# Attention on one core: scores of two tiles in one batch, and the shares divided by their sums in rows on GpSimd

## What is computed

```python
for window, dilation in DILATED_PATTERNS:      # (128, 1), (512, 4), (2048, 16)
    o_i, lse_i = dilated_window_attn(q, k, v, window, dilation)
    ...
mix_w = jax.nn.softmax(jnp.stack(lses, axis=0), axis=0)
o = jnp.sum(mix_w[..., None] * jnp.stack(outs, axis=0).astype(jnp.float32), axis=0)
attn_out = o.astype(x.dtype).reshape(B, S, ATTN_WIDTH) * jax.nn.silu(g_attn)
```

## Time and profile before

| | |
|---|---|
| median of 3 runs | 2517.62 us (2516.89 to 2519.19) |
| the profiled execution's own time | 2515.38 us |
| its span, first to last instruction | 2513.4 us |
| busy in the span: PE, DVE, ACT, POOL | 97%, 51%, 44%, 25% |
| attention, first score product to last gate | from 479.66 us, last gate starts at 609.45 us and takes 0.69 us |
| busy from 480 to 600 us: PE, DVE, ACT, POOL | 118.85, 72.48, 79.35, 42.16 us of 120 |

### The profile page before, as it was taken

One profiled execution on the slowest core, in us unless ns is written; L12 is line 12 of the kernel. 1 busy time (PEld: TensorE's weight loads), 2 busy tenths in 40 slices (PEclk: granted clock), 3 DMA queues, 4 the chain that ended last, 5 costly groups with the idle time before them and its releaser, 6 DMA issues. The chain is left out here.

```text
span 2513.4 us, 31851 instructions
## 1 busy us (share of the span) xinstructions
PE 2439.6 (97%) x12866; PEld 2019.2 (80%) x12866; DVE 1285.0 (51%) x1582; ACT 1097.3 (44%) x1569; POOL 616.2 (25%) x497
## 2 busy tenths in 40 slices
PE   8899999999999999999999998999999999999997
PEld 7788888766878788888888777877888888888885
DVE  5654102254521312213554286335269998888985
ACT  5510221365333121121422265233237877877783
POOL 0121232142412122133231056314111114312100
PEclk9999999999999999999999999999999999999999
DMA  7732321242232113113242374222548999999996
GB/s 287 271 107 84 107 75 54 89 129 83 92 101 67 34 34 134 51 59 127 68 134 59 126 276 175 102 70 67 182 186 365 386 377 396 393 384 376 379 376 242
DMA packets 138299, 446.47 MB, mean 178 GB/s; under 512 B 20952, under 2 KB 63640, under 8 KB 121512
## 3 DMA queue, kind: packets, MB, share of 16 engines
q1 hardware_dynamic: 96304, 380.23, 40.5%
q0 software_dynamic: 15632, 36.29, 3.9%
q10 hardware_dynamic: 26216, 27.89, 3.4%
HBM read 385.06 MB, written 77.14 MB: 184 GB/s over the span
## 5 line engine op out<-in xcount | busy, mean ns | idle before, releaser
L3220 DVE TENSOR_TENSOR ex_w_lo<-ex_w,ex_w_hi 128x2048 fp32r<-128x2048 f32 x198 | 447.4, 2289 | 55.0 <-ACT ex_w_hi L3156 53.7
L3156 ACT ACTIVATE ex_w_hi<-ex_w 128x2048 fp32r<-128x2048 f32 x198 | 376.9, 1916 | 34.6 <-DMA ex_w<-w 19.8
L249 POOL TENSOR_TENSOR p_w_lo<-w_raw,p_w_hi 128x512 fp32r<-128x512 f32 (+1 forms) x138 | 181.7, 1348 | 593.2 <-ACT p_w_hi L275 592.4
L316 PE MATMUL p_ps<-hT_hi,p_w_hi 128*128 128x512 f32 (+1 forms) x608 | 218.7, 360 | 3.5 <-DVE p_w_lo L249 3.3
L317 PE MATMUL p_ps<-hT_lo,p_w_hi 128*128 128x512 f32 (+1 forms) x608 | 217.3, 357 | 0.0
L318 PE MATMUL p_ps<-hT_hi,p_w_lo 128*128 128x512 f32 (+1 forms) x608 | 217.2, 357 | 0.0
L275 ACT ACTIVATE p_w_hi<-w_raw 128x512 fp32r<-128x512 f32 (+1 forms) x200 | 112.4, 607 | 218.3 <-PE p_ps L318 88.2
L249 POOL TENSOR_TENSOR p_w_lo_rest<-w_raw,p_w_hi_rest 128x512 fp32r<-128x512 f32 x64 | 86.8, 1391 | 207.1 <-ACT p_w_hi_rest L275 207.1
L316 PEld LDWEIGHTS p_ps<-hT_hi,p_w_hi 128*128 128x128 f32 x608 | 116.1, 191 | 21.4 <-DVE hT_lo L715 3.4
L318 PEld LDWEIGHTS p_ps<-hT_hi,p_w_lo 128*128 128x128 f32 x608 | 116.0, 191 | 16.3
L317 PEld LDWEIGHTS p_ps<-hT_lo,p_w_hi 128*128 128x128 f32 x608 | 116.0, 191 | 16.2
(11 more groups left out here) (525 smaller groups left out, 6005.2 us busy)
## 6 DMA issues: line engine op xcount, KB each, us to landing
ex_w<-w SPq DMA_DIRECT2D x99, 2048.0 KB, 14.5
w_raw<-w_in SPq DMA_DIRECT2D x36, 1024.0 KB, 5.2
w_raw<-w_xkv_panels SPq DMA_DIRECT2D x8, 1024.0 KB, 7.0
w_raw<-w_out SPq DMA_DIRECT2D x8, 1024.0 KB, 8.6
x_rows<-o_x SPq DMA_DIRECT2D x16, 512.0 KB, 2.6
qk_columns<-ml_qk_first ACTq DMA_DIRECT2D x16, 512.0 KB, 3.2
w_raw<-w_qk_panels SPq DMA_DIRECT2D x6, 1024.0 KB, 7.7
plain_cols<-x SPq DMA_DIRECT2D x8, 512.0 KB, 7.3
```

Source lines behind the costliest of these rows:

```text
L249: emit(self.lo(n)[:, 0:w], self.half(n // (KC // 2), w)[:, n % (KC // 2), :], self.hi(n)[:, 0:w].bitcast(F32), ALU.subtract).then_inc(self ...
L316: pe.matmul(out, a, x, start=start, stop=False)
L3156: nc.scalar.activation(w_hi[:, n % RING, :], raw_half(n), ACT.Copy).then_inc(hi_done, 1)
L3220: nc.vector.tensor_tensor(w_lo[:, n % RING, :], raw_half(n), w_hi[:, n % RING, :].bitcast(F32), ALU.subtract).then_inc(down_lo if m == "w2 ...
```

## The change

Two things are changed in attention.

First, steps of kind "rows" now cover two tiles (n and n + 1). TensorE makes the near products of both tiles and then the far products of both. The steps stand at other places: ahead of units 0 and 1 for tiles 4-5 and 6-7, ahead of units 3 and 4 for tiles 0-1 and 2-3 of the next pair.

Second, the kind "sums" is gone, with spread_sums, keep_scales, scale, and the buffer att_scales (its place in memory stays taken, so nothing else moves). Each tile's shares are instead divided in rows: invert takes the reciprocals of two tiles, 4 columns at a time, and a new function normalize on GpSimd multiplies each row of att_sc by its reciprocal, in place, four instructions for two tiles. turn waits for them (normed) instead of for the exponentials (expd).

```diff
+    NORMED_BEHIND = {1: HALF, 2: HALF + 2, 4: NT, 6: NT + 2}
...
-        for a in range(HALF):
+        for a in range(0, HALF, 2):
             yield "rows", a
         for hp in range(PAIRS):
             for u in range(PER):
-                if u < 3:
-                    yield "rows", NT * hp + HALF + u
-                elif hp + 1 < PAIRS and u != PER - 2:
-                    yield "rows", NT * (hp + 1) + (u - 3 if u < PER - 2 else u - 4)
-                if u == PER - 1 and hp + 1 < PAIRS:
-                    yield "rows", NT * (hp + 1) + HALF - 1
+                if u in (0, 1):
+                    yield "rows", NT * hp + HALF + 2 * u
+                if u in (3, 4) and hp + 1 < PAIRS:
+                    yield "rows", NT * (hp + 1) + 2 * (u - 3)
                 yield "block", PER * hp + u
-                if u == 2:
-                    yield "rows", NT * hp + NT - 1
-                    yield "sums", 2 * hp
-                if u == PER - 2:
-                    yield "sums", 2 * hp + 1
...
             def _(pool):
-                def scale(d):
-                    pool.wait_ge(scales_kept, d + 1)
-                    nc.gpsimd.tensor_tensor(columns(d), scales[:, d % 2, :], columns(d), ALU.mult).then_inc(scaled, 1)
+                def normalize(i):
+                    pool.wait_ge(inverted, i // 2 + 1)
+                    for a in (i, i + 1):
+                        for k in range(2):
+                            nc.gpsimd.tensor_scalar(row_of(a, k), row_of(a, k), rden[:, 2 * a + k:2 * a + k + 1], None,
+                                                    ALU.mult).then_inc(normed, 1)
 
                 for kind, n in items():
-                    if kind == "sums":
-                        scale(n)
-                    if kind == "block" and n % 2 == 0 and 2 <= n <= 32:
-                        next_weights.prepare(pool, n // 2 - 1, n // 2)
+                    if kind == "rows" and n < HALF:
+                        normalize(n)
+                    if kind == "block":
+                        hp, u = divmod(n, PER)
+                        if u in NORMED_BEHIND and NT * hp + NORMED_BEHIND[u] < NT * PAIRS and n > 0:
+                            normalize(NT * hp + NORMED_BEHIND[u])
+                        if n % 2 == 0 and 2 <= n <= 32:
+                            next_weights.prepare(pool, n // 2 - 1, n // 2)
...
+                    q, keys = qk[hp % 2][:, 0, :], qk[hp % 2][:, 1, :]
+                    for m in range(2):
+                        if i >= 2:
+                            pe.wait_ge(maxed, 2 * (i + m - 1))
...
+                    for m in range(2):
+                        if FAR[a + m]:
...
                 def turn(n, k):
                     hp, u, half, rows, pieces, far = unit(n)
                     if k == 0:
-                        pe.wait_ge(expd, 2 * rows_before(n))
+                        pe.wait_ge(normed, 2 * rows_before(n))
...
                 def gate(d):
-                    dve.wait_ge(scaled, d + 1)
                     dve.wait_ge(summed, PER * (d // 2) + (PER if d % 2 else FIRST[1]))
...
+                late = []
                 for kind, n in items():
                     if kind == "rows":
-                        if late is not None:
-                            maxes(late, 1)
+                        for x in late:
+                            maxes(*x)
                         maxes(n, 0)
-                        late = n
+                        maxes(n, 1)
+                        late = [(n + 1, 0), (n + 1, 1)]
+                        if n == HALF - 2:
+                            invert(0)
                     if kind == "block":
                         hp, u = divmod(n, PER)
...
                         keep(n)
+                        for x in late:
+                            maxes(*x)
+                        late = []
+                        if u in NORMED_BEHIND and NT * hp + NORMED_BEHIND[u] < NT * PAIRS and n > 0:
+                            invert(NT * hp + NORMED_BEHIND[u])
```

More of the change, by code:

```diff
@@ L918, in attention @@
         scored, maxed, expd = c.sem("att_scored"), c.sem("att_maxed"), c.sem("att_expd")
-        inverted, spread, scales_kept, scaled = (c.sem(f"att_{n}") for n in ("inverted", "spread", "scales_kept", "scaled"))
+        inverted, normed = c.sem("att_inverted"), c.sem("att_normed")
         turned, kept = c.sem("att_turned"), [c.sem(f"att_kept{k}") for k in range(2)]
@@ L988, in scores @@
                         pe.wait_ge(qk_in[hp % 2], 32 * (hp // 2 + 1))
[L989 to L1002, removed]
@@ L1003, in scores @@
-                    ins.then_inc(scored, 1)
+                    q, keys = qk[hp % 2][:, 0, :], qk[hp % 2][:, 1, :]
+                    for m in range(2):
+                        if i >= 2:
+                            pe.wait_ge(maxed, 2 * (i + m - 1))
+                        for k in range(2):
+                            at = slice(HD * k, HD * k + HD)
+                            ins = pe.matmul(bank_of(i + m, k)[:, FAR[a + m]:], q[at, (a + m) * P:(a + m + 1) * P],
+                                            keys[at, (a + m + 1) * P - NEAR[a + m]:(a + m + 1) * P], start=True, stop=True)
+                        if not FAR[a + m]:
+                            ins.then_inc(scored, 1)
@@ new lines, in scores @@
+                    for m in range(2):
+                        if FAR[a + m]:
+                            runs = keys[:, 0:STRIDE * FAR[a + m]].rearrange("p (u r a) -> p r u a", r=STRIDE, a=RUN)
+                            for r in range(STRIDE):
+                                for k in range(2):
+                                    at, rows = slice(HD * k, HD * k + HD), slice(RUN * r, RUN * r + RUN)
+                                    own = slice((a + m) * P + RUN * r, (a + m) * P + RUN * r + RUN)
+                                    ins = pe.matmul(bank_of(i + m, k)[rows, 0:FAR[a + m]], q[at, own], runs[at, r],
+                                                    start=True, stop=True)
+                            ins.then_inc(scored, 1)
@@ L1014, in turn @@
                     ins.then_inc(turned, 1)
-                def spread_sums(d):
-                    pe.wait_ge(inverted, d + 1)
-                    if d >= 1:
-                        pe.wait_ge(gated, d)
-                    for r in range(HALF):
-                        for k in range(2):
-                            at = NT * d + 2 * r + k
-                            ins = pe.matmul(ps_o[HD * k:HD * (k + 1), 1 - d % 2, r * P:(r + 1) * P],
-                                            rden[:, at:at + 1].to_broadcast([P, HD]), c.const("ident"),
-                                            start=True, stop=True)
-                    ins.then_inc(spread, 1)
                 def values(n):
@@ L1065, in _ @@
                         scores(n)
-                    elif kind == "sums":
-                        spread_sums(n)
                     else:
@@ L1144, in keep @@
                     nc.scalar.activation(pT[0:w, n % RING, 1, 0:wide], ps_t[0:w, 1, 0:wide], ACT.Copy).then_inc(kept[1], 1)
-                def keep_scales(d):
-                    act.wait_ge(spread, d + 1)
-                    if d >= 2:
-                        act.wait_ge(scaled, d - 1)
-                    nc.scalar.activation(by_position(scales[:, d % 2, :]), by_run(ps_o[:, 1 - d % 2, :]), ACT.Copy
-                                         ).then_inc(scales_kept, 1)
-                late = None
+                late = []
                 for kind, n in items():
-                    if late is not None and (kind == "rows" or kind == "block" and late < rows_before(n)):
-                        exps(late)
-                        late = None
                     if kind == "rows":
-                        late = n
-                    if kind == "sums":
-                        keep_scales(n)
+                        for x in late:
+                            exps(*x)
+                        exps(n, 0)
+                        late = [(n, 1), (n + 1, 0), (n + 1, 1)]
                     if kind == "block":
                         keep(n)
-                        if late is not None:
-                            exps(late)
-                            late = None
+                        for x in late[:2]:
+                            exps(*x)
+                        late = late[2:]
 def out_weights(c, stack, tag, w):
```

42 lines of the change are left out of this document (14 added, 28 removed).

## The result

The changed kernel takes 2554.12 us (median of 4 runs, 2550.25 to 2556.64), the kernel before 2517.26 us beside it (4 runs, 2514.12 to 2519.19). The ratio is 1.015, 95% interval 1.0137 to 1.0162: 37 us slower. The prediction was 2514.3 us with a range of 2507.6 to 2529.6. The profiled execution's span is 2554.8 us, 41.4 us more than before. Its attention stage goes from 478.10 us to 648.62 us, 170.5 us against 130.5 before, so 40.0 of these 41.4 us lie in it. (The profiled execution is the slowest of the four.)

The account below looks back on a forecast made before the run. PE's list was taken to bound the attention stage: 19.3 us off it and 16.0 us of added waits gave -3.3 us, so 2517.62 - 3.3 = 2514.3 us, range 2507.6 to 2529.6.

Parts of the forecast that it names:

- the price of the added instruction: GpSimd's 96 multiplications between exponentials and turns: 0.53 us each for 384 columns, 0.59 for 448.
- the copy's line: Line through GpSimd's one-operand copies, 0.29 us for 128 columns and 0.61 for 512, giving 0.56 us for 448.
- PE's wait at unit 3: PE's turn of unit 3 waits for the division of tiles 4 and 5: 0.97 us, 1.81 in the last pair.
- GpSimd too slow: Rival: at 1.14 us for 448 columns GpSimd becomes the bound; +19 us, 2537. Slow cases +0.5 to +20: 22%.
- The rule that spoke against the change: Trainium skill: GpSimd wrong for ordinary elementwise work, VectorE about twice as fast; twice its 0.618 us gives 1.24 us.
- The clock: Rival: waits up to 1.8 us in the last pair might lower PE's granted clock; 1 to 2 us, counted in ranges.
- PE's list: PE's attention work falls by 19.3 us: 11.4 from spread sums, 7.9 from batches.
- Spread sums: PE's products spreading the sums, removed by the change: six pairs at 1.90 us, 11.4 us saved.
- The waits for maxes: PE's scores wait for VectorE's maxes (att_negmax), foretold at about 9 us in the changed profile.
- Tile 7's wait: PE waits 0.86 us for VectorE's maxes before tile 7's scores, in every pair from the second on.
- The reload: GpSimd's library reload before its first multiplication: taken as nothing; the skill's 6 us would make the sum 0.5 us worse.
- wrong if: Signs against the forecast: multiplications over 0.7 us, no waits at unit 3, or first turn later than 487 us.

Follow-up runs that it names:

- constant_factor: The changed kernel with the constant 0.125 in place of the reciprocal as factor of all 96 GpSimd multiplications; one run, 2551.7 us.
- chunks_apart: The changed kernel with the 16 chunks of the next weights on GpSimd moved behind units 2, 4 and 6 of each pair; ratio 1.0133 to the kernel before.
- batches_only: The kernel before with only the two-tile scores and the new order of maxes and exponentials, sums still spread by products; ratio 0.9991 to the kernel before.
- no_division: The changed kernel without the 96 GpSimd multiplications, turns waiting for the exponentials; 2498.27 us against 2514.01 for the kernel before.
- half_dose: The changed kernel with only head 0's 48 multiplications on GpSimd, head 1's shares not divided; 2513.56 us against 2514.06 for the kernel before.
- scalar_and_gpsimd: The changed kernel with head 0's multiplications as two-operand products on GpSimd, head 1's as scaled copies on ScalarE; 2505.74 us against 2514.63 for the kernel before.

## Why the prediction was wrong

- **The step that failed** is the price of the added instruction: "I take the copy's line and 0.03 us for the factor, my choice: 0.53 us for 384, 0.59 for 448." It measured 1.25 and 1.41 us, 2.4 times as much, and lies even above the line through the two-operand product (1.14) that was the upper bound. That "a multiplication by one number per partition reads one row like the copy" did not carry over to its time; constant_factor shows that the form costs, with or without a factor to read. What followed from the price has its place right and its size wrong: the four multiplications of tiles 4 and 5 took 4.90 us where 1.99 was laid out, and PE's wait at unit 3 became 3.54 us instead of 0.97.
- **The rival that happened** was named: GpSimd too slow, with the break-even at 0.68 us. The measured prices fall on its side in order: 0.93 us gave +13 us, 1.41 us gave +37. But its price was capped at 1.14 us and +19 us, and its chance at 22%. It had GpSimd as the bound and 32 us of waits for it; PE waited 31.8 us, with GpSimd busy for 101 of 120 us and itself waiting for reciprocals.
- **The rule that spoke against the change** was put aside. Twice VectorE's time gave 1.24 us, nearer to 1.41 than the 0.59 taken from the copy. That nearness is in part luck: the time doubled was that of a max, and VectorE's own one-factor multiplication took 0.39 us for 448 columns, so GpSimd's is some 3.6 times as long. The other half of that rule (the Trainium skill, GPSIMD Engine Reference, Engine selection: one input at roughly line rate) is not borne out by this form: 448 columns took 0.93 us with two inputs and 1.41 with one.
- **The clock** was put at 1 to 2 us for waits of up to 1.8 us. The wait at unit 3 was 1.7 us in the first pair, 3.5 in the next four and 4.1 in the last, and the price some 3 to 7 us. Not every such wait was followed by a slow turn: in chunks_apart the turn behind a wait of 3.30 us, at 553.23, took its usual 1.09 us.
- **PE's list** was right for its parts together. Spread sums 11.4 us, and with the batches 14.8 us net of the waits for maxes; the stage without the division measured 14.7, and 11.3 of it lie between batches_only and no_division. Two far groups of 64 columns took 0.46 us listed, 0.39 without the usual overlap of 0.07; 0.38 was foretold.
- **The waits for maxes** were right in place and under half the size: 3.9 us listed in place of about 9. Tile 7's wait was 0.36 us (571.70), or 0.43 from start to start, where 0.86 was expected. So the lists were some 1 to 5 us too pessimistic for the stage in the runs in which GpSimd is not the bound (half_dose, no_division, batches_only, scalar_and_gpsimd).
- **The reload** of GpSimd's library cost nothing: its first multiplication starts at 482.19 us, as soon as the reciprocal is there. The first turn stands at 485.25 us, inside the 487 foretold.
- Of the signs written down as "wrong if", one came true, multiplications of over 0.7 us. Of the other things foretold for the profile, a pair was to take 20 to 20.8 us and took 27.2, and the last gate was to start near 606 us and started at 647.93.

What stays open is how the 30 us or so beyond the clock's price divide between the chain and the loop it closes (slower turns make later scores, later reciprocals and a later start of the next chain), and why the one-factor form is slow on GpSimd.

## What to carry to other kernels

An instruction that no row shows is not priced by the row that it resembles in what it reads; when the forecast's sign turns within the bounds (here at 0.68 us between 0.59 and 1.14), the case beyond the turning point deserves more than a fifth of the chances, or the instruction a run of its own. Work put on an engine with idle time still costs when it stands in a chain that the bound engine waits for: judge it by the chain's length per pair, not by the engine's busy share. And a plan that loses may need only another engine for the same work: half on ScalarE and half on GpSimd, there in the two-operand form, turned +37 us into -10.

## What the hardware showed unexpectedly

- GpSimd, one-factor multiplication in SBUF, fp32: 0.60 us for 128 and 1.41 for 448 columns, 2.5 ns a column; the product with the factor spread over the columns: 0.40 and 0.93 us, 1.7 ns a column.
- VectorE's one-factor multiplication: 0.39 us for 448 columns alone, 1.14 us in the mean with GpSimd at work beside it. ScalarE's copy with a scale took 0.66 us for 448 columns, as its exponential over the same columns did, and GpSimd's product beside it kept 0.93.
- VectorE's reciprocal, fp32: 3.35 us for 512 columns, 0.17 us for 4.
- TensorE fell to 1.2 GHz (granted clock 0.50) after waits of 3.5 us inside attention: near products 2.08 us at 556.21, turns 1.97 us at 559.38 and 1.85 at 563.18, each near twice its time. With products in the waits the turns of unit 3 shown took 1.09 us and the mean granted clock was 0.97 instead of 0.82.
